# A decoder layer with expert retrieval: TensorE spreads the norm weights over the partitions and adds the chunk bias, and norm2's weights are applied to the transposed rows of h

## The reference

```python
def rmsnorm(x, g):
    xf = x * lax.rsqrt(jnp.mean(x * x, axis=-1, keepdims=True) + EPS)
    return xf * g
# n = rmsnorm(x, norm1_g); n @ w_in -> q, k, v, u, vc, qm, gates
vc = rmsnorm(gelu(vc), chunk_norm_g)
s = jnp.einsum('gts,bnsgc->bntgc', tril(ws), vc) + bs      # chunk branch, bias by position
a_chunk = gelu(u) * s
h = x + sum(sigmoid(gates + b_gate) * branch_projections) @ w_out
n2 = rmsnorm(h, norm2_g)
q = n2 @ wq                     # 8 heads x 2 halves x 128
# top 16 of 128 sub-keys per half, top 16 of the pairs: 8 x 16 experts per token
y = h + sum_k softmax(score)_k * gelu(n2 . peer_u[e_k]) * peer_v[e_k]
y = rmsnorm(y, final_norm_g)
```

## Time and profile before

| | us |
|---|---|
| median of 3 runs | 3373.37 (3368.38 to 3374.26) |
| the profiled execution | 3373.66 |
| its span | 3371.9 |
| TensorE, VectorE, ScalarE, GpSimd busy | 2811.1, 2491.4, 711.7, 2123.3 |
| bytes moved | 1317.05 MB |

### The profile page before, as it was taken

One profiled execution on the slowest core, in us unless ns is written; L12 is line 12 of the kernel. 1 busy time (PEld: TensorE's weight loads), 2 busy tenths in 40 slices (PEclk: granted clock), 3 DMA queues, 4 the chain that ended last, 5 costly groups with the idle time before them and its releaser, 6 DMA issues.

```text
span 3371.9 us, 31005 instructions
## 1 busy us (share of the span) xinstructions
PE 2811.1 (83%) x9134; PEld 1579.4 (47%) x9134; DVE 2491.4 (74%) x5834; ACT 711.7 (21%) x1826; POOL 2123.3 (63%) x2128
## 2 busy tenths in 40 slices
PE   8988998899898988979877788878887777777775
PEld 6866685645454543535544555533443333333320
DVE  2277876789898888768888777767877667777764
ACT  2232211221411112222222111111221211221211
POOL 0045655556776666666677666667667777777775
PEclk9999999999999998989987799989998889989988
DMA  8779999999999999999999999999999999999998
GB/s 313 287 292 368 363 401 396 406 382 407 365 405 410 411 406 402 403 402 395 407 395 409 409 410 410 410 406 392 406 399 396 410 409 409 404 400 407 409 392 321
DMA packets 374295, 1317.05 MB, mean 391 GB/s; under 512 B 37984, under 2 KB 42848, under 8 KB 374112
## 3 DMA queue, kind: packets, MB, share of 16 engines
q0 software_dynamic: 304608, 1108.41, 83.5%
q1 hardware_dynamic: 69520, 206.66, 15.9%
HBM read 1303.64 MB, written 12.26 MB: 390 GB/s over the span
## 4 chain that ended last, share of the span: by engine, by line
POOL 28%; PE 22%; DMA 21%; issue 14%; DVE 13%; ACT 2%; DVEq 0%; POOLq 0%; SPq 0%; ACTq 0%
DMA v_ring_sb<-peer_v,i_all_sb 15%; POOL u_ring_sb L1958 14%; POOL v_ring_sb L1970 14%; PE ps L1271 8%; DVE u_ring_sb L1859 5%; PE ps L1182 4%; DMA u_ring_sb<-peer_u,i_all_sb 3%; DVE h_buf_sb L1873 2%; PE ps L947 2%; PE ps L1187 2%; PE ps L1218 2%; PE ps L1197 2%; PE ps L965 1%; DMA v_ring_sb<-peer_v,i_packed_sb 1%; ACT area_sb L1354 1%
## 5 line engine op out<-in xcount | busy, mean ns | idle before, releaser
L1271 PE MATMUL ps<-v_ring_sb,diag_sb 128*128 128x512 f32 x2712 | 1395.6, 667 | 422.4 <-DMA v_ring_sb<-peer_v,i_all_sb 380.2
L1958 POOL DMA_INDIRECT u_ring_sb<-peer_u,i_all_sb x1024 | 1029.8, 1006 | 740.8 <-DVE u_ring_sb L1859 286.1
L1859 DVE SCALAR_TENSOR_TENSOR u_ring_sb<-u_ring_sb,ps 128x1024 f32<-128x1024 f32 x1056 | 1252.2, 1216 | 244.5 <-DMA u_ring_sb<-peer_u,i_all_sb 211.6
L1970 POOL DMA_INDIRECT v_ring_sb<-peer_v,i_all_sb x1024 | 1026.3, 1002 | 455.7 <-issue 277.4
L1271 PEld LDWEIGHTS ps<-v_ring_sb,diag_sb 128*128 128x128 f32 x2712 | 560.3, 213 | 1166.3 <-issue 633.3
L1873 DVE SCALAR_TENSOR_TENSOR h_buf_sb<-v_ring_sb,c_sb,h_buf_sb 128x1024 f32<-128x1024 f32 x346 | 444.7, 1285 | 275.3 <-DMA v_ring_sb<-peer_v,i_all_sb 253.4
L1490 ACT ACTIVATE diag_sb<-ident_sb,c_sb 128x128 f32<-128x128 f32 x678 | 226.0, 392 | 1401.2 <-DVE c_sb L1869 1385.4
L1182 PE MATMUL ps<-xnT_sb,w_ring_sb 128*128 128x256 f32 (+3 forms) x1280 | 328.7, 410 | 1.6 <-DVE feats_sb L1657 1.6
L1182 PEld LDWEIGHTS ps<-xnT_sb,w_ring_sb 128*128 128x128 f32 x1280 | 234.1, 191 | 99.5 <-issue 28.3
L1218 PE MATMUL ps<-xnT_sb,w_ring_sb 128*128 128x256 f32 (+3 forms) x896 | 222.0, 407 | 5.2 <-DMA w_ring_sb<-w_q 4.4
L1218 PEld LDWEIGHTS ps<-xnT_sb,w_ring_sb 128*128 128x128 f32 x896 | 162.7, 194 | 67.0 <-issue 11.0
(11 more groups left out here) (266 smaller groups left out, 2123.2 us busy)
## 6 DMA issues: line engine op xcount, KB each, us to landing
w_ring_sb<-w_d SPq DMA_DIRECT2D x40, 1536.0 KB, 10.5
w_ring_sb<-w_q SPq DMA_DIRECT2D x14, 2048.0 KB, 20.3
w_ring_sb<-w_b SPq DMA_DIRECT2D x10, 2048.0 KB, 14.7
u_ring_sb<-peer_u,i_all_sb POOLq DMA_INDIRECT x1024, 14.1
v_ring_sb<-peer_v,i_all_sb POOLq DMA_INDIRECT x1024, 14.2
w_ring_sb<-w_out SPq DMA_DIRECT2D x6, 2048.0 KB, 19.8
feats_sb<-x SPq DMA_DIRECT2D x12, 512.0 KB, 23.2
u_ring_sb<-w_d SPq DMA_DIRECT2D x4, 1536.0 KB, 7.1
```

Of the source, the lines that this page charges most:

```text
L1271: last = mm(ps[0:M, half, :], diag[:, n % 2, j, 0:M], v_ring[:, n % 2, j, half * 512:(half + 1) * 512], start=opens, stop=closes)
L1859: V.add(v.scalar_tensor_tensor(u, u, 1.0, n2_cur[:, :], ALU.mult, ALU.mult, accum_out=act4[:, n % 2, j:j + 1]), dots, NB * n + j + 1)
L1958: g.indirect_dma_start(u_ring[:, n % 2, j, :], None, t["peer_u"], index(n, j)).then_inc(u_in[n % 2][j], 16)
L1970: g.indirect_dma_start(v_ring[:, n % 2, j, :], None, t["peer_v"], index(n, j)).then_inc(v_in[n % 2][j], 16)
```

## The change

Eight things are done; line numbers of the changed kernel stand in the order rows only.

1. `norm2_g`, `final_g` and `chunk_b` are no longer loaded on all partitions. Three small DMAs on POOL's queue (`ROWS`) bring them as 8, 8 and 4 rows of 128 into unused partitions of `ws_T_smp`.
2. A new unit `grow` spreads them: TensorE multiplies 8 rows with a column of the identity repeated 128 times, 4 matmuls for each half, 8 for 1024 columns, into two banks. There is one before each tile's first batch (`norm2`) and one before its end (`final`), 18 in all. `start_tile` and `finish` read the banks, in two halves of 512 columns.
3. In `spatial` TensorE adds the bias by one more matmul for each channel group, and VectorE's add (L1584) is gone. For the sample tile the eight matmuls wait for one another.
4. `norm_h` no longer multiplies; TensorE transposes h itself, without waiting for VectorE's product, and `turn_h` moves from ScalarE to VectorE, where it multiplies with norm2's weights by column. These come from one more transpose in `values` of tile 0. The order is now `square_h`, `turn_h`, `norm_h`.
5. `costs` is changed to match, so the planner places the front of the later groups anew; `smp_mem` must not come before step 131 (before: 122).
6. For the last group the queries go to `q_last` in the space of `feats`, one copy each instead of two; ScalarE waits for the stores of h before the first.
7. Gates, blocks and queries get an index s of the group's share. There is one share in each group, so nothing follows from it; the weight slots stay the same too.
8. The dump of squares is written as bytes, two scratch areas move.

```diff
@@ front_units
     out += [("square_h", t) for t in tiles]
+    out += [("turn_h", t) for t in tiles]
     out += [("norm_h", t) for t in tiles]
-    out += [("turn_h", t) for t in tiles]
@@ costs
-                out=(7.0, 0.7), turn_h=(2.0, 0), ... norm_h=(0, 2.2),
+                out=(7.0, 0.7), turn_h=(2.0, 1.4), grow=(2.2, 0), ... norm_h=(0, 0.9),
@@ not_ahead_of
+    if u == ("smp_mem", 0):
+        return [BATCHES * 4 + 3]
@@ build_steps
+    for x in range(TILES):
+        if x:
+            at[BATCHES * x - 1].append(("grow", "norm2", x))
+        else:
+            at[0].insert(0, ("grow", "norm2", x))
+        at[BATCHES * (x + 1) + 2 if x < PTILES else TOTAL - 2].append(("grow", "final", x))
@@ loads
-        SECOND = dict(chunk_g=chunk_g, ws_T=ws_T, ws_T_smp=ws_T_smp[0:SAMPLE], chunk_b=chunk_b,
+        SECOND = dict(chunk_g=chunk_g, ws_T=ws_T, ws_T_smp=ws_T_smp[0:SAMPLE],
-        CONSTS = dict(subT=subT, norm2_g=norm2_g, final_g=final_g)
+        CONSTS = dict(subT=subT)
@@ tensor, values
+                if x == 0:
+                    tr(ps[:, 1, 0:DC], norm2_rows, ident[96:96 + DC, 96:96 + DC]).then_inc(columns_mm, 1)
@@ tensor, spatial
-                    last = mm(bank("spatial", x)[:, c * P:c * P + R], vc[0:R, k, c * P:(c + 1) * P], w, start=True, stop=True)
+                    last = mm(to, vc[0:R, k, c * P:(c + 1) * P], w, start=True, stop=False)
+                    if R == P:
+                        last = mm(to, ident[32:32 + CG, 32 + c:33 + c].broadcast_to([CG, P]), chunk_rows, start=False, stop=True)
@@ tensor, turn_h
-                pe.wait_ge(n2_ready, x + 1)
+                for h in range(2):
+                    pe.wait_ge(*gone("out", x, h))
@@ tensor, new
+            def grow(kind, x):
+                rows, first = (norm2_rows, 96) if kind == "norm2" else (final_rows, 64)
+                for h in range(2):
+                    pe.wait_ge(*free("grow", kind, x, h))
+                    for c in range(4):
+                        at_c = first + 4 * h + c
+                        last = mm(bank("grow", kind, x, h)[:, c * P:(c + 1) * P],
+                                  ident[first:first + DC, at_c:at_c + 1].broadcast_to([DC, P]), rows, start=True, stop=True)
+                    last.then_inc(f_mm, 1)
@@ scalar, query
+                if n == 0 and s == 0:
+                    for m in range(1, MOST):
+                        act.wait_ge(h_stored[m], h_stores(g, m))
@@ vector, spatial
-                    V.add(v.tensor_tensor(gated, bank("spatial", x)..., chunk_b[:, :, :], ALU.add), *left("spatial", x))
-                V.add(v.tensor_tensor(feats[:, FU:FU + CG, W], feats[:, FU:FU + CG, W], gated[:, :, 0:R], ALU.mult), u_ready, x + 1)
+                V.add(v.tensor_tensor(feats[:, FU:FU + CG, W], feats[:, FU:FU + CG, W],
+                                      bank("spatial", x).rearrange("p (c n) -> p c n", c=CG)[:, :, 0:R], ALU.mult),
@@ vector, norm_h and turn_h
-                V.add(v.tensor_tensor(n2[k][0:R, :], h_new(x), norm2_g[0:R, :], ALU.mult), n2_ready, x + 1)
+                for h in range(2):
+                    dve.wait_ge(f_mm, upto("nturn", x, h))
+                    V.add(v.tensor_tensor(xnT[:, 4 * h:4 * h + 4, W], bank("nturn", x, h)...,
+                                          wide(norm2_col[:, 4 * h:4 * h + 4], 4, R), ALU.mult), *left("nturn", x, h))
@@ vector, start_tile
-                V.add(v.scalar_tensor_tensor(n2_cur[:, :], h_buf[:, x % 2, :], root_h[:, x:x + 1], norm2_g[:, :], ALU.mult, ALU.mult))
+                for h in range(2):
+                    dve.wait_ge(f_mm, upto("grow", "norm2", x, h))
+                    V.add(v.scalar_tensor_tensor(n2_cur[:, part], h_buf[:, x % 2, part], root_h[:, x:x + 1],
+                                                 bank("grow", "norm2", x, h), ALU.mult, ALU.mult), *left("grow", "norm2", x, h))
```

323 lines of the change are left out of this document (188 added, 135 removed).

## The result

The changed kernel takes 3397.4 us (median of 4 runs, 3390.8 to 3401.1) against 3373.1 before. The ratio of the two is 1.0072, with a 95% interval from 1.0058 to 1.0086: some 24 us, 20 to 29. The forecast was 3371.5 with a range from 3360 to 3383.

The account below looks back on a forecast made before the run. The prediction took DMA bytes at about 410 GB/s to bound the kernel after the first gather. Its terms, -0.2 + 0.2 - 2 + 0 + 0.1 = -1.9, led from 3373.66 to 3371.8, stated as 3371.5 us, range 3360 to 3383.

Parts of the forecast that it names:

- New matmuls: Bias and grow matmuls at 0.265 us each, 0.136 as low end; 48 us more TensorE work in all.
- Up to the first gather: TensorE's chain before the first u gather at 201.6 us: sum -0.2 us, between -1.4 and +0.2.
- the load of `chunk_b`: Dropped 0.26 MB load while TensorE waits for w_vvc: gain taken as 0.3 us, up to 0.96.
- The relief behind the last add of h: From the last add of h to the first query: 2.2 us instead of 3.27, a gain of 1.06 us.
- Step 0: Query 11 waits for start_tile's first half, delaying the first v gather: +0.2 us, from 0 to +1.
- The plan of group 1: New plan removes half the dry time at 285 to 380 us, later front gives part back: -2, -5 to +5.
- The one long wait for the gelu: Batch 5's gelu at 302.45 us, VectorE waiting 12.70: forecast at about 298, wait under 8 us.
- Groups 2 and 3, batches, tail: Later scores 0 (-4 to +4), group 3 0, batches 0 (at most +3), tail +0.1 us; steps stay 10.24 us.
- Rival (3): TensorE becomes the bound in group 1's front, and all later work shifts: +10 us, 3383; chance 0.15.
- Rival (2): The smoother plan removes most dry time: -13 us, 3360; chance 0.26.
- Rival (4): An engine, not DMA, sets the pace everywhere: +40 us, 3413; chance 0.02.

Follow-up runs that it names:

- i4_before_bias128: Kernel before, with the bias done by TensorE over 128 rows, chunk_b not loaded and no VectorE add: 3373.7 us, ratio 1.0007.
- i1: Changed kernel with 128 rows in the bias matmuls and without grow, norm2_g and final_g loaded on all partitions again: 3368.8 us, ratio 0.9992.
- h1: Changed kernel with 128 rows in the bias matmuls only, grow still on 8 rows: 3375.2 us, ratio 1.0015.
- i2: Kernel before, with 32 added matmuls over 4 rows of zeros between those of spatial, adding nothing to the result: 3392.5 us, ratio 1.0059.
- i3: Kernel before, with the same 32 added matmuls as i2 but over 128 rows: 3376.1 us, ratio 1.0016.
- e2_plan: Kernel before, with the changed kernel's plan and no instruction added or taken away: 3376.0 us, ratio 1.0014.
- e1_room: Changed kernel with the planner's room search started at the kernel before's 16.9 and 14.2 us instead of 10.0: 3402.7 us, ratio 1.0092.
- e3_late: Changed kernel with only tile 0's norm2 grow moved from ahead of query 9 to behind query 11: 3390.7 us, ratio 1.0062.
- e4_both: Changed kernel with the edits of e1_room and e3_late together: 3399.7 us, ratio 1.0087.
- h3_fulllate: Changed kernel with 128 rows in all added matmuls and tile 0's norm2 grow behind query 11: 3372.4 us, ratio 1.0004.
- f1_full: Changed kernel with the same matmuls, those of the bias and grow over 128 rows instead of 4 and 8: 3375.8 us, ratio 1.0014.
- j2_rows4_twice: Kernel before, with eight matmuls of 4 rows in a row ahead of each tile's full ones in spatial, results overwritten: 3388.5 us, ratio 1.0055.

## Why the prediction was wrong, step by step

**From the kernel before to the changed one** a chain of runs leads, in us by the ratios: bias on TensorE over 128 rows +2 (`i4_before_bias128`), the plan, the new `turn_h` and the small parts together -5 (`i1` against `i4`), `grow` +8 (`h1` against `i1`), and 4 rows instead of 128 in the bias +19 (the changed kernel against `h1`). These add up to 24 by their construction; the first two steps are hardly clear of noise. The last is borne out apart from the chain by `i2` against `i3`, 14 us in the kernel before. The plan can't be priced alone: it costs the kernel before 5 us (`e2_plan`), and in the changed kernel it is 7 us better than the old one (`e1_room`), with intervals that overlap.

- **New matmuls: this step failed.** "I take 0.265, as they are matmuls" was right for `grow` (its 144 matmuls kept TensorE busy for 36.8 us, forecast 38) and wrong for the bias, not in the duration of one but in what 4 rows do to their neighbours. The price was taken from a stretch in which all matmuls have 128 rows, and the clock was counted nowhere; in the sum the bias stood only with tile 0's 1.06 us, and groups 1 to 3 had no term for it. To the 9.5 us of TensorE's time for the bias come, as an estimate, 12 us by the slower pace (8 pairs a tile, 0.41 - 0.22 = 0.19 us each, 8 tiles) and 15 us by the half clock (30.7/2). What the total paid for 4 rows instead of 128 is 19 us. Both bounds that I kept for one matmul, 0.136 and 0.265, were bounds for its duration, and the loss lay outside it. With 128 rows the change measures 1.0015, +5 us instead of the forecast -2, and within the range.
- **Up to the first gather: right in the sum, by luck.** It came at 201.68 (forecast 201.4, before 201.60). But the four bias matmuls of tile 0, forecast at 1.06 us, made `spatial` 2.3 us longer (3.2 instead of 0.9), and the projection ahead of it ended 1.5 us sooner (its wait for `w_vvc` was 0.4 us shorter and its 16 instructions 1.1), against 0.3 forecast for the load of `chunk_b`. Besides, in `e1_room`, `e3_late` and `e4_both`, whose list of units is the same up to step 0, the first gather came at 205.79, 203.74 and 202.92 us: executions spread over 4 us here, more than any of these terms. The relief behind the last add of h came as computed: VectorE's add ends at 177.72 and the query starts at 179.95, 2.2 us:

```profile
177.03 0.69 DVE L1831 SCALAR_TENSOR_TENSOR h_buf_sb<-ps,h_buf_sb 128x512 f32<-128x512 f32 x1 [6.17 <-PE ps L1291]
...
179.95 3.32 PE L1325 MATMUL ps<-xnT_sb,w_ring_sb 128*128 128x128 f32 x16 [1.06 <-issue]
```

- **Step 0: the wait was right, its price was not.** +0.2 was forecast and the gather is 2.4 us late; TensorE's chain ended at 222, not 219. The step took query 11's duration at the full clock, though its 16 instructions came right behind 6.85 us of waiting: 211.38 to about 214.9 are 3.5 us and not 1.86. Moving `grow` away is worth 3 us by the ratios, between two kernels with 128 rows as well (`h3_fulllate` against `f1_full`, 10.2 instead of 13.3 us from the first u to the first v gather), so this term of the sum was some 2 us too small.
- **The plan of group 1: right mechanism, wrong balance.** -2 was forecast, within -5 and +5; the plan alone, in the kernel before, measured +5. The two stretches in `e2_plan`:

```profile
285.00:380.00 95.00, 80.99 (x312) 52.47 (x311) 78.09 (x175) 34.49 (x102) 58.56 (x56) 0.91 0.96 361
380.00:580.00 200.00, 186.92 (x729) 137.98 (x727) 146.03 (x276) 22.99 (x59) 102.89 (x103) 0.96 1.00 384
```

By the measure used above, 285 to 380 us lose 10.9 instead of 17.5 us, a little more than the 5 us of relief that were forecast, and 380 to 580 us lose 11.8 instead of 3.9: there the later front gives back more than it got. The one long wait for the gelu became two, as forecast at under 8 us each (VectorE in the changed kernel, in brackets the wait):

```profile
292.32 0.17 DVE L1978 TENSOR_TENSOR c_sb<-gelu_sb,g_all_sb 128x4 f32<-128x4 f32 x1 [4.60 <-ACT gelu_sb L1610]
...
307.85 0.16 DVE L1978 TENSOR_TENSOR c_sb<-gelu_sb,g_all_sb 128x4 f32<-128x4 f32 x1 [6.61 <-ACT gelu_sb L1610]
```

- **Groups 2 and 3, batches, tail:** the equal steps of the last third are still 10.24 us apart and lose nothing:

```profile
2803.52 1.22 DVE L1968 SCALAR_TENSOR_TENSOR u_ring_sb<-u_ring_sb,ps 128x1024 f32<-128x1024 f32 x1 [1.94 <-DMA u_ring_sb<-peer_u,i_all_sb]
...
2813.76 1.22 DVE L1968 SCALAR_TENSOR_TENSOR u_ring_sb<-u_ring_sb,ps 128x1024 f32<-128x1024 f32 x1 [2.39 <-DMA u_ring_sb<-peer_u,i_all_sb]
```

- **The rivals.** Rival (3), TensorE as the bound in front of group 1, came true in kind, at 24 us instead of 10: by the table above +13.0 in group 1 and +6.8 in group 2, and most of it for a reason that it did not name. It was held down by "TensorE had 81.43 of 95 us", a mean over a stretch in which the front's chain has no slack. Rival (2), the plan as a gain of 13 us, did not come true: `e2_plan` has +5, and at most 7 or 8 us of gain stand in the changed kernel (`e1_room`, `e4_both`). Rival (4) is refuted by the stretch from 2440 us on, where TensorE is busy for 18 us more and nothing more is lost. `grow`'s 38 us cost 8, a fifth: the prediction counted only the one in step 0.

## What to carry to other kernels

A matmul that contracts over few rows and stands among full ones should be given all 128 rows, if a column of the identity or rows of zeros make it possible: it takes no longer and here it was worth 19 of 24 us. Where that can't be, put a few such matmuls together: four in a row in each tile cost the kernel before 8 us instead of the 20 of the mixed order, but eight in a row cost 19. When work is added to TensorE, cost its neighbours too: the pace from start to start, and the granted clock in the stretch behind, not the duration of one instruction.

## What the runs showed of the hardware that I had not expected

- Matmuls (pairs of instructions) that alternate between 128 rows and 4 or 32 rows start 0.41 us apart, matmuls over 128 rows 0.22 us, at the full clock. Eight matmuls of 4 rows in a row take 759.03 - 757.05 = 1.98 us in `j2_rows4_twice`, 0.25 each.
- TensorE's granted clock fell to 0.50 though the engine was busy without a gap: before the fall at 774.4 us it had done 4-row and 128-row matmuls in turn. In the four places it stayed there for 3.4 to 10.2 us at a time; at the longest the next block took 8.28 instead of 5.33 us.
- The same matmuls over 128 rows, as long each (275 ns an instruction, against 270 at the least over 4 rows), left it at 1.00 in the same places (`h1_fullbias`, `f1_full`, `i3_before_rows128`).
